# Gathering expert inputs from x1 in float32 instead of three bfloat16 parts, with a weight ring of twelve pieces instead of nine and the router's tail in another order

## The reference, cut to what matters

```python
x = x + jnp.einsum('bse,ed->bsd', mixed, w_out[l])        # x1
h = rmsnorm(x, norm2_g[l])                                # x1 / rms * g2
logits = jnp.dot(h, w_router) + b_router                  # 256 x 32
top_v, top_e = lax.top_k(logits, 4)
gates = jax.nn.softmax(top_v, axis=-1)
# for each expert e, on its tokens xb:
gu = jnp.dot(xb, w_gate_up[e]) + b_gate_up[e]             # 1024 x 2048
gate = jnp.minimum(gu[:, :1024], 7.0)
up = jnp.clip(gu[:, 1024:], -7.0, 7.0)
act = gate * jax.nn.sigmoid(1.702 * gate) * (up + 1.0)
y = jnp.dot(act, w_down[e]) + b_down[e]                   # 1024 x 1024
# the result is x1 plus the sum of gate * y over a token's experts
```

## Time and profile before

| | before |
|---|---|
| median of 3 runs | 1094.94 us (1093.09 to 1095.05) |
| profiled execution, its own time | 1094.92 us |
| its span | 1093.2 us |
| PE busy | 1030.3 us (94%) |
| PE weight load busy | 408.5 us (37%) |
| DVE, ACT, POOL busy | 189.7, 125.7, 11.2 us |
| DMA | 424.57 MB, mean 388 GB/s |

### The profile page before, as it was taken

One profiled execution on the slowest core, in us unless ns is written; L12 is line 12 of the kernel. 1 busy time (PEld: TensorE's weight loads), 2 busy tenths in 40 slices (PEclk: granted clock), 3 DMA queues, 4 the chain that ended last, 5 costly groups with the idle time before them and its releaser, 6 DMA issues.

```text
span 1093.2 us, 14242 instructions
## 1 busy us (share of the span) xinstructions
PE 1030.3 (94%) x5955; PEld 408.5 (37%) x5955; DVE 189.7 (17%) x470; ACT 125.7 (11%) x264; POOL 11.2 (1%) x23
## 2 busy tenths in 40 slices
PE   9999999999999999999999999999999999999997
PEld 5755564333333333333323333333333333233332
DVE  2143333011111111111001111111111110111111
ACT  2034431000100000000000000000000000000000
POOL 1000010000000000000000000000000000000000
PEclk9999999899999999999999999999999999999999
DMA  9942655899999999999999999999999999999995
GB/s 347 356 188 78 245 222 232 365 428 427 428 427 430 427 428 428 427 428 429 428 427 428 428 428 428 428 427 429 427 429 428 428 428 428 427 429 426 427 427 239
DMA packets 40191, 424.57 MB, mean 388 GB/s; under 512 B 6304, under 2 KB 7368, under 8 KB 15464
## 3 DMA queue, kind: packets, MB, share of 16 engines
q1 hardware_dynamic: 40152, 424.23, 92.6%
q10 hardware_dynamic: 16, 0.00, 0.0%
HBM read 423.18 MB, written 1.05 MB: 388 GB/s over the span
## 4 chain that ended last, share of the span: by engine, by line
PE 59%; DMA 39%; DVE 1%; issue 0%; ACT 0%; DVEq 0%; SPq 0%
DMA ring<-in_w_gate_up 35%; PE bank L1425 20%; PE bank L1456 14%; PE bank L1113 5%; PE bank L1397 4%; DMA ring<-in_w_down 4%; PE bank L1371 3%; PE bank L1299 3%; PE bank L1413 2%; PE bank L1443 1%; PE bank L1135 1%; PE bank L1147 1%; PE bank L1434 1%; PE bank L1185 1%; PE bank L1386 0%
## 5 line engine op out<-in xcount | busy, mean ns | idle before, releaser
L1425 PE MATMUL bank<-ring,ht 128*64 128x512 f32 x2048 | 455.9, 596 | 49.5 <-DMA ring<-in_w_gate_up 49.3
L1425 PEld LDWEIGHTS bank<-ring,ht 128*64 128x64 f32 x2048 | 139.1, 137 | 364.1 <-issue 263.9
L1456 PE MATMUL bank<-ring,ht 128*64 128x512 f32 x1024 | 229.3, 600 | 2.5 <-DMA ring<-in_w_down 2.5
L1050 DVE TENSOR_SCALAR mix_t<-bank 128x512 f32<-128x512 f32 x32 | 22.1, 692 | 763.9 <-PE bank L1425 763.9
L1456 PEld LDWEIGHTS bank<-ring,ht 128*64 128x64 f32 x1024 | 71.3, 138 | 157.3 <-issue 133.3
L1397 PE MATMUL bank<-ht,hn 64*128 64x512 f32 x256 | 71.7, 639 | 0.7 <-ACT ht L741 0.7
L725 ACT ACTIVATE hn<-bank 128x256 f32<-128x256 f32 x32 | 12.3, 384 | 516.1 <-PE bank L1434 516.1
L1113 PE MATMUL bank<-ring,ht 128*128 128x512 f32 x128 | 58.9, 600 | 0.0
L1371 PE MATMUL bank<-pick,parts 128*128 128x64 bf16 x1536 | 50.0, 193 | 0.0
L1371 PEld LDWEIGHTS bank<-pick,parts 128*128 128x128 bf16 x1536 | 49.1, 98 | 0.3
L741 ACT ACTIVATE ht<-bank 128x512 f32<-128x512 f32 x32 | 19.1, 597 | 245.6 <-PE bank L1456 245.6
(11 more groups left out here) (194 smaller groups left out, 395.0 us busy)
## 6 DMA issues: line engine op xcount, KB each, us to landing
ring<-in_w_gate_up SPq DMA_DIRECT2D x128, 2048.0 KB, 37.2
ring<-in_w_down SPq DMA_DIRECT2D x64, 2048.0 KB, 40.2
ring<-in_w_in SPq DMA_DIRECT2D x5, 2048.0 KB, 15.7
ring<-in_w_out SPq DMA_DIRECT2D x1, 4096.0 KB, 13.4
ring<-in_w_in SPq DMA_DIRECT2D x2, 1024.0 KB, 8.5
ring<-in_attn_bias SPq DMA_DIRECT2D x1, 1536.0 KB, 18.8
xres<-in_x SPq DMA_DIRECT2D x2, 512.0 KB, 3.8
out<-xres SPq DMA_DIRECT2D x4, 256.0 KB, 2.2
```

The source lines that it names most:

```text
L1050: dve.tensor_scalar(gate_c, bank[0][:, :], LIMIT, None, ALU.min).then_inc(gate_cut, 1)
L1425: mm = pe.matmul(bank[h][c * CAP:(c + 1) * CAP, :], xe_t[:, k, :], w[:, k % RUN, at:at + BANK], start=False, stop=(k == KD - 1), skip_grou ...
L1456: mm = pe.matmul(bank[6][c * CAP:(c + 1) * CAP, :], turned[:, at:at + CAP], w[:, k % DRUN, c * BANK:(c + 1) * BANK], start=(k == 0), stop= ...
```

## The change

It does four things.

1. `gather` reads `xres` (x1 in float32) instead of the three parts: 16 float32 matmuls instead of 48 bfloat16 ones for each expert. `pick` is float32 and holds 1/rms (`rs2`) in place of one. The work that made the parts (ACT, POOL, DVE) is gone.
2. The ring has 12 pieces. The room comes from `hn`, `attn_tmp`, `ht` and `mix_t`, which now lie in pieces 9 and 11, from the parts, and from buffers that share their place. A lap of the loops is two experts, not three; `brow` and `s_sb` have two buffers, not three. SP issues four gate_up pieces of expert 1 during the dense part (two of them after `half_mixed`), and its two down pieces after `mixed` and after `logits`.
3. The router's tail: token tile 0 goes through maximum, index, comparison and mask before tile 1; the rank matrix adds 1000 for a taken expert (so `pos` is a copy); ranks and picks come ahead of the gates; `gather(0)` comes ahead of the gates' transposes; `keep_warm` before the ranks has 4 matmuls, not 12, and the 2 matmuls stand between the ranks.
4. In expert 0 both halves of `start_sum` come ahead of the activation's transposes.

```diff
-PIECES = 9
+PIECES = 12
-LAP = 3
-LAPS = 9
+LAP = 2
+LAPS = 14
-WARM = (12, 2, 12, 2)
+WARM = (12, 2, 4, 2)
...
-        ring = sb("ring", [P, (PIECES + 1) * PIECE])
+        ring = sb("ring", [P, PIECES * PIECE])
...
-        hn = sb("hn", [P, T, D])
+        hn_flat = ring[:, 9 * PIECE:9 * PIECE + T * D]
...
-        parts = sb("parts", [P, T, 3, D], BF16)
...
+            sp.wait_ge(half_mixed, 1)
+            load_gu(1, 2, 8)
+            sp.wait_ge(m_num, HM)
+            load_gu(1, 3, 9)
             sp.wait_ge(mix_m, HM)
             sp.dma_start(bdn, b_down[0]).then_inc(ld_bdn, 16)
             sp.wait_ge(mixed, 4)
-            load_gu(1, 2, 8)
+            load_d(1, 0, 10)
+            sp.wait_ge(logits, T)
+            load_d(1, 1, 11)
...
+            def take(e):
+                for t in range(T):
+                    ins = dve.tensor_scalar(pick[:, t, :], slot[:, 0:CAP], pos[:, t, bass.ds(e, 1)], rs2[:, t:t + 1],
+                                            ALU.is_equal, ALU.mult)
...
+            rank = bank[ACC[2]]
             pe.wait_ge(mask_ready, 1)
-            pe.matmul(bank[0][:, 0:NE], before[:, :], mask[:, 0, :], start=True, stop=True)
-            pe.matmul(bank[0][:, NE:2 * NE], ones[:, :], mask[:, 0, :], start=True, stop=False)
-            pe.matmul(bank[0][:, NE:2 * NE], before[:, :], mask[:, 1, :], start=False, stop=True).then_inc(ranks, 1)
+            pe.matmul(rank[:, 0:NE], before, mask[:, 0, :], start=True, stop=True)
+            pe.matmul(rank[:, NE:2 * NE], ones[:, :], mask[:, 0, :], start=True, stop=False)
             keep_warm(WARM[3])
...
+            pe.wait_ge(mask_ready, 2)
+            pe.matmul(rank[:, NE:2 * NE], before, mask[:, 1, :], start=False, stop=True).then_inc(ranks, 1)
...
-                        for i in range(3):
-                            q, j = k // RUN, k % RUN
-                            rows = parts[:, t, i, q * RUN * P:(q + 1) * RUN * P].rearrange("p (m j) -> p j m", j=RUN)[:, j, :]
-                            mm = pe.matmul(bank[7][:, k * CAP:(k + 1) * CAP], rows, pick[:, t, :],
-                                           start=(t + i == 0), stop=(t == T - 1 and i == 2))
+                        q, j = k // RUN, k % RUN
+                        rows = xres[:, t, q * RUN * P:(q + 1) * RUN * P].rearrange("p (m j) -> p j m", j=RUN)[:, j, :]
+                        mm = pe.matmul(bank[7][:, k * CAP:(k + 1) * CAP], rows, pick[:, t, :],
+                                       start=(t == 0), stop=(t == T - 1))
...
                 if meanwhile:
                     meanwhile(0)
+                    meanwhile(1)
...
+            gather(0)
+            pe.wait_ge(gates_ready, 1)
+            for t in range(T):
+                mm = pe.transpose(bank[6][0:NE, t * P:(t + 1) * P], gate[:, t, :], ident[:, :])
+            mm.then_inc(gate_turned, 1)
+            pe.wait_ge(pmax_ready, 1)
+            pe.transpose(bank[ACC[3]][0:1, 0:P], pmax[:, :], ident[:, :]).then_inc(pmax_turned, 1)
             experts(0, 0, start_sum)
```

More of the change, by code:

```diff
@@ L100 @@
 PIECE_LOADS = [len(range(s, KINDS * NE, PIECES)) for s in range(PIECES)]
-TINT_LOADS = [sum(tint(n) == u for n in range(NE)) for u in range(3)]
+TINT_LOADS = [sum(tint(n) == u for n in range(NE)) for u in range(len(TINT))]
 def tints_before(n):
@@ L138, in in_second_half @@
             place[0] += words
-            assert place[0] <= 2 * half
+            assert place[0] <= 8 * PIECE
             return ring[:, at:at + words]
@@ L183, in layer_kernel @@
         sq_x = attn_tmp[:, 0:D]
-        brow = attn_tmp[:, 0:3 * BANK].rearrange("p (u n) -> p u n", u=3)
-        om = sb("om", [P, T, HALF])
-        bdn = om[0:NE, :, :].rearrange("p t n -> p (t n)")
+        ht = ring[:, 11 * PIECE:11 * PIECE + KD * SEQ].rearrange("p (k n) -> p k n", k=KD)
+        mix_flat = ring[:, 11 * PIECE + KD * SEQ:12 * PIECE]
+        mix_t = mix_flat.rearrange("p (k n) -> p k n", k=KD)
+        rows_i, rows_f, rows_l, rows_b, ones_r = (mix_flat[0:HM, i * SEQ:(i + 1) * SEQ] for i in range(5))
@@ new lines, in layer_kernel @@
+        gate_t = s_sb[0:NE, 1, :]
+        brow = sb("brow", [P, len(TINT), BANK])
+        pickg = sb("pickg", [P, T, 2 * CAP])
+        pick = sb("pick", [P, T, CAP])
+        gate_buf = sb("gate_c", [P, BANK])
+        gate_c = gate_buf[:, :]
+        wif = gate_buf[:, 0:KD * 2 * HM].rearrange("p (k n) -> p k n", k=KD)
+        vec_r = gate_buf[0:ROWS, KD * 2 * HM:KD * 2 * HM + P]
+        if_c = gate_buf[:, P + KD * 2 * HM:P + (KD + T) * 2 * HM].rearrange("p (t s h) -> p t s h", t=T, s=2)
+        eq, eqg = (gate_buf[:, i * T * TOPK * NE:(i + 1) * T * TOPK * NE].rearrange("p (t j e) -> p t j e", t=T, j=TOPK)
+                   for i in range(2))
@@ L223, in layer_kernel @@
         rs2 = sb("rs2", [P, T])
-        lg = sb("lg", [P, T, NE])
-        top_v = sb("top_v", [P, T, 8])
+        lg, mask = (sig_buf[:, i * T * NE:(i + 1) * T * NE].rearrange("p (t e) -> p t e", t=T) for i in range(2))
+        top_v = sig_buf[:, 2 * T * NE:2 * T * NE + T * 8].rearrange("p (t e) -> p t e", t=T)
         top_i = sb("top_i", [P, T, 8], U32)
-        top_f = sb("top_f", [P, T, TOPK])
         nv0 = sb("nv0", [P, T])
@@ L256, in layer_kernel @@
         ld_wm = sem("ld_wm")
-        ld_wout = sem("ld_wout")
+        ld_wout = [sem(f"ld_wout{i}") for i in range(2)]
         ld_bdn = sem("ld_bdn")
@@ L260, in layer_kernel @@
         ld_g2 = sem("ld_g2")
-        ld_brow = [sem(f"ld_brow{i}") for i in range(3)]
+        ld_brow = [sem(f"ld_brow{i}") for i in range(len(TINT))]
         pool_step = sem("pool_step")
@@ L332, in layer_kernel @@
         mix_m = sem("mix_m")
+        half_mixed = sem("half_mixed")
         mixed = sem("mixed")
@@ L457, in free_of, with next_gu @@
                 return gu_used, GUN * base + GUN * m + was + 1
[L459 to L463, removed]
-                for h in range(first, GUN):
+            def next_gu(base, far, n):
+                sp.wait_ge(brow_used, base + far + n - 1)
+                load_brow(far + n, tint(n))
+                for h in range(GUN):
                     used, count = free_of(base, n, h)
@@ L677, in square_x @@
                 act.wait_ge(x1_ready, 2 * t + c + 1)
-                act.activation(hn[:, t, c * BANK:(c + 1) * BANK], xres[:, t, c * BANK:(c + 1) * BANK], ACT.Square,
+                if t + c:
+                    act.wait_ge(x1_ss, 2 * t + c)
+                else:
+                    act.wait_ge(m_ss, T * HM)
+                act.activation(squares, xres[:, t, c * BANK:(c + 1) * BANK], ACT.Square,
                                accum_out=ss2h[:, t, c:c + 1]).then_inc(x1_ss, 1)
@@ L1001, in _ @@
+            take(0)
             dve.wait_ge(top_exp, T)
@@ L1415, in gate_up @@
                 mm.then_inc(brow_used, 1)
+            def gate_up(base, lap, n, round_no):
+                now = base + LAP * lap + n
+                tinted(base, lap, n, round_no)
                 pe.wait_ge(xe_ready, now + 1)
@@ L1472, in expert @@
                 turn_act(now, bank[6])
-                if meanwhile:
-                    meanwhile(1)
-                else:
+                if not meanwhile:
                     spread(now - 1, tint(n - 1 if n else NE - 1), 1)
```

231 lines of the change are left out of this document (85 added, 146 removed).

## The result

| | before | changed |
|---|---|---|
| median | 1094.99 us (1093.09 to 1095.91, 4 runs) | 1108.09 us (1106.75 to 1108.88, 4 runs) |
| profiled execution, its own time | 1094.92 us | 1106.75 us |
| its span | 1093.2 us | 1105.0 us |

The ratio is 1.0121, 95% interval 1.0103 to 1.0138: the change makes the kernel slower by 13.1 us.

What follows compares the result with a forecast made beforehand. PE was to bound the kernel from the start: expert 1 at 211.1, 29 experts of 28.37, 58.4 for the end and 1.8 for expert 30's gather give 1094.0, with 1.72 around the span 1095.5 us; range 1083 to 1112.

Steps and rivals of the forecast that it cites:

- Part 1: The ring: three more pieces bring the last awaited transfer 14.8 us earlier; a later stall moves to PE.
- the sum: Whole kernel: 211.1 + 29 x 28.37 + 58.4 + 1.8 = 1094.0 us; PE never waits for a piece.
- Part 2: The gather in each expert: 3.58 us, 2.1 more; PE's wait absorbs 0.2 to 0.3, so an expert grows by 1.8.
- rival (c): The gather's load pays for its step: slower from 0.114 us an instruction, 1104 at 0.12, 1161 at 0.18; chance 0.14.
- Part 3: Up to expert 0: clock stays at 1.2 GHz, gather takes 6.8 us, first gate_up starts near 175.0 instead of 171.16.
- Part 4: Expert 0: takes 36.1 us instead of 31.6, so expert 1 starts at 211.1 instead of 202.76.
- Rival (a): Before expert 0: the clock comes back at 166 as before, 6.5 us less, 1089.0; chance 0.17.
- (b): The gather is hardly dearer, or hides, and the transfers bound as before: 1082 us; chance 0.07.
- (d): The clock falls in each expert between gate_up and down: 26 us more, 1121; chance 0.07.
- the ring's gain: Three more pieces at 4.92 us each, 14.8 us; end at 1078.4 if nothing else changed.

Runs made afterwards that it cites:

- experiment 3: The kernel before (nine pieces, old tail) with only the float32 gather and float32 picks holding 1/rms: 1112.2 us against 1096.59, ratio 1.0137.
- experiment 2: The changed kernel gathering only token tile 0, 16 instructions instead of 32: 1083.77 us against 1096.59 for the kernel before, ratio 0.9883.
- experiment 5: The changed kernel with gather operands exchanged (picks loaded, x1 moved, plus a copy and four transposes): 1077.3 us against 1095.22 for the kernel before, ratio 0.9838.
- experiment 1: The changed kernel with the gather's loads reading 128 adjacent columns of x1, without a step: 1101.43 us against 1096.59 for the kernel before, ratio 1.0054.
- experiment 4: The changed kernel with 12 warm matmuls ahead of the ranks instead of 4: 1103.55 us against 1096.59 for the kernel before, ratio 1.0083.
- experiment 6: The changed kernel with the edits of experiment 5 and experiment 4 together: 1079.76 us against 1095.22 for the kernel before, ratio 0.9848.

## Why the prediction was right or wrong

The forecast was 1095.5, PE-bound, within 0.2% of before; it is 1108.09, slower by 1.2%, inside the range (1083 to 1112) and outside the forecast's own (1090 to 1101).

**The bound was right.** The pace is constant from expert 1 to 29, there is no wait for a piece, and PE bounds from the start, as Part 1 and the sum say; experiment 3 shows it apart from the ring, experiments 2 and 5 that the transfers bound again at a pace of 26.9 or 27.4. By Part 1's times the last weights were to land two pieces behind 1062, at 1072; they do near 1070.6.

**The step that failed is the pace of Part 2**, 28.37 instead of 28.80. It was mis-sized in two terms of equal size:
- The gather: 32 x 0.112 = 3.58 us against 3.81. Experiment 1 gives 0.19 of it to the step of two elements (0.118 against 0.111 a load). This is rival (c), which was to decide for slower by itself from 0.114 on: it came true at its middle price, 0.12, the interval of the transposes' loads, and not at the 0.18 that adds the whole difference of two durations.
- What PE's wait for the activation would absorb: 0.2 to 0.3 us against 0.08. I had put the sum's four matmuls at 0.96 us, and they take 1.06; the idle 0.84 of the load for L1443 was for the most part the time in which the sum's matmuls ran with their weights already loaded. In the changed kernel, where PE no longer waits there, the same load still stands idle for 0.76 us. An idle load is not an idle PE. The rows at hand showed it: the loads had ended at 246.06 - 0.84 = 245.22, the sum's four matmuls at 244.92 + 1.13 = 246.05.

Together 0.43 x 29 = 12.5 us; with 1.6 less at the start and 0.1 more at the end that makes 11.0: the difference of the spans, 1105.0 against 1094.0. The rest to the median is that the profiled execution was the fastest of four.

In the gather a step of two costs 6 ns of 112 (experiment 1). In the transposes a load lasts 141 ns without a step and 209 at a step of two (experiment 5), no less than the 210 at a step of four. The Trainium skill (SBUF — State Buffer, Door 1: The DMA port swizzle) lets two hits on a 16-byte line be enough for full rate. By these rows it is not so: two elements a line cost a little in the gather, and in the transposes as much as one element a line.

**Parts 3 and 4, the start,** were right in outline: I said half a clock between 165 and 180 us, and it was so from 165.8 to 176.1; first gate_up at 175.0 against 171.7, expert 1 at 211.1 against 209.5. That the second is so close is partly luck, since two errors offset each other. What failed in Part 3 is when the clock falls: I had taken over from before that it is low already from 160 on, so the gather was to take 6.8 us and took 5.44, and gate_up started 3.3 us early. In Part 4 expert 0 took 37.7 us, not 36.1: the clock fell again during L1344, the bias of down, and stayed low into the next stretch (0.66 between 190 and 200 us, as before, but 0.83 instead of 1.00 between 200 and 210), where I had put 0.9 less. Rival (a) would have been worth the 4.8 us of experiment 4, not 6.5, and would not have made the kernel faster. Whether warm matmuls hold the clock stays open: they go with full clock in experiments 4 and 6, but in experiment 3 it fell behind the same 28 instructions.

**Rivals (b) and (d)** fell. (b), that the gather hides and the transfers bound as before, came about with PE at 26.9 and 27.4 an expert (experiments 2 and 5), not at 28.80. (d), a clock that falls in each expert, did not happen: from expert 1 on gate_up takes 13.88 us, and down 7.02, as at full clock.

**Where the ring's gain went:** nowhere in the changed kernel, for the last weights come 8 us earlier (1070.6 against 1078.5) and PE, with no time to spare left, can't use them. PE alone with the old gather would have ended at 1031.7; the new one takes 2.23 us more in each of 30 experts, 67 us, where PE had 61.5 to spare, and expert 1 starts 6.7 later (209.50 against 202.76): 1105.4, against a span of 1105.0.

## What to carry to other kernels

An engine that waits 60 us in all has 2 us to spare in each of 30 rounds; divide the slack by the rounds before you spend it, and give each term of a round's sum to the hundredth. Where the load of the stationary operand is the price of a float32 matmul, as in this gather with its 64 moving columns, try the narrow matrix as the stationary one, even if that adds a copy and transposes: here 2.43 us of PE instead of 3.81. A larger buffer gives nothing while its consumer is the limit: test it and a slower consumer each with the other undone.

## What the runs showed of the hardware that was not expected

- In the gather a float32 load of 128 columns takes 0.111 us back to back and 0.118 with a step of two elements (experiment 1); 16 fewer matmul instructions of 64 columns save 0.1175 each, the load and nothing else (experiment 2).
- The load of a float32 transpose lasts 141 ns without a step, 209 at a step of two (experiment 5) and 210 at a step of four.
- Four matmuls of 64 stationary columns with 512 moving float32 columns each, two in each half of the array's columns, are 8 instructions and take 1.86 us, 0.23 each (experiment 5); gate_up's 64 of that shape take 13.88, 0.217 each.
- Where the clock falls is not settled by the warm matmuls alone. With 12 instructions of `keep_warm` it fell at 165.8, during the gather, in the changed kernel, and during the logits (0.95 between 155 and 160) in experiment 5. With 28 it stayed full up to gate_up in the profiles of experiments 4 and 6, and fell at 165.8 in experiment 3, where PE had waited 1.53 us for the mask before the ranks. The two slower runs of experiment 4 have no profile; their mean granted clock (0.991 against 0.995) says that it was low for longer, not where.
